# A layer of a hybrid encoder on one core: operand stores issued ahead of the next chunk's loads in mixing, another order of work where the stages of the feed-forward phase change, and POOL making the held operand's sums for the first two blocks of each later stage

## The reference

```python
def mixer(x, mem, w_in, conv_w, conv_b, conv_ln_g, conv_ln_b, pool_w, pool_scale, w_mk, w_mv, w_out):
    h = x @ w_in
    ...
    a = jax.nn.silu(layer_norm(a, conv_ln_g, conv_ln_b))   # GLU, causal depthwise conv of width 31
    p = pool_mixer(p_in, pool_w, pool_scale)
    mo = memory_cross_attention(q, mem, w_mk, w_mv)
    return jnp.concatenate([a, p, mo], axis=-1) @ w_out

def conv_ffn(x, w_up, ffn_conv_w, ffn_conv_b, w_down):
    u = causal_depthwise_conv(x @ w_up, ffn_conv_w, ffn_conv_b)   # width 3
    g = u[..., :D_FF]
    v = u[..., D_FF:]
    return (jax.nn.silu(g) * v) @ w_down                           # D_FF = 2816

x = layer_norm(x, ln0_g, ln0_b)
x = layer_norm(DEEPNORM_ALPHA * x + mixer(x, ...), ln1_g, ln1_b)
x = layer_norm(DEEPNORM_ALPHA * x + conv_ffn(x, ...), ln2_g, ln2_b)
```

## Time and profile before

| | us |
|---|---|
| median of three runs | 2126.25 |
| lowest and highest | 2125.7, 2127.76 |
| the profiled execution | 2126.83 |
| its span, first to last instruction | 2125.1 |
| PE busy in it | 1924.2 (91%) |
| DVE busy | 1627.2 (77%) |
| ACT busy | 984.3 (46%) |
| POOL busy | 220.7 (10%) |

### The profile page before, as it was taken

One profiled execution on the slowest core, in us unless ns is written; L12 is line 12 of the kernel. 1 busy time (PEld: TensorE's weight loads), 2 busy tenths in 40 slices (PEclk: granted clock), 3 DMA queues, 4 the chain that ended last, 5 costly groups with the idle time before them and its releaser, 6 DMA issues.

```text
span 2125.1 us, 26517 instructions
## 1 busy us (share of the span) xinstructions
PE 1924.2 (91%) x8584; PEld 1585.8 (75%) x8584; DVE 1627.2 (77%) x2241; ACT 984.3 (46%) x1681; POOL 220.7 (10%) x263
## 2 busy tenths in 40 slices
PE   4999999679788919999999989999999798998997
PEld 3887877558677717888888768888888586887885
DVE  7979868567677637888888888877778767657897
ACT  4255252554554325555555655555555434324321
POOL 1010100001131210222221002000000000000111
PEclk9999999889899959999999999999999899999998
DMA  6130210523224253333434433322214467557542
GB/s 251 57 119 20 79 40 21 195 75 132 106 104 148 101 217 124 139 135 131 148 138 138 167 131 129 109 89 79 84 74 137 167 216 267 172 175 259 188 165 102
DMA packets 135378, 282.96 MB, mean 133 GB/s; under 512 B 10384, under 2 KB 66832, under 8 KB 135312
## 3 DMA queue, kind: packets, MB, share of 16 engines
q1 hardware_dynamic: 135312, 282.13, 37.4%
HBM read 182.48 MB, written 99.61 MB: 133 GB/s over the span
## 4 chain that ended last, share of the span: by engine, by line
PE 54%; DMA 4%; DVE 3%; ACT 1%; issue 1%; SPq 0%; POOL 0%; DVEq 0%; ACTq 0%; POOLq 0%
PE prod_ps L1662 54%; DVE mov_lo L1837 1%; DMA y_scratch<-up_and_out 1%; ACT mov_hi L1709 1%; DMA mov_raw<-wdown_sums_scratch 1%; DMA mov_raw<-in_w_down 1%; DMA mov_raw<-x_operands 1%; DVE up_and_out L1871 0%; DMA ffn_conv_b<-in_ffn_conv_b 0%; DVE up_and_out L1868 0%; DMA up_and_out<-x_scratch 0%; DVE sta_lo L1833 0%; ACT sta_hi L1702 0%; SPq L1489 0%; DVE sta_raw L1849 0%
## 5 line engine op out<-in xcount | busy, mean ns | idle before, releaser
L1662 PE MATMUL prod_ps<-mov_hi,sta_hi 128*128 128x512 f32 x1848 | 727.8, 394 | 46.1 <-ACT half_sums L1722 22.3
L1662 PE MATMUL prod_ps<-mov_lo,sta_hi 128*128 128x512 f32 x1848 | 725.2, 392 | 0.0
L1662 PE MATMUL prod_ps<-mov_hi,sta_lo 128*128 128x512 f32 x1848 | 724.5, 392 | 0.0
L1662 PEld LDWEIGHTS prod_ps<-mov_hi,sta_hi 128*128 128x128 f32 x1848 | 350.7, 190 | 126.9 <-ACT half_sums L1722 24.7
L1662 PEld LDWEIGHTS prod_ps<-mov_hi,sta_lo 128*128 128x128 f32 x1848 | 350.6, 190 | 73.7
L1662 PEld LDWEIGHTS prod_ps<-mov_lo,sta_hi 128*128 128x128 f32 x1848 | 351.0, 190 | 72.5
L1702 ACT ACTIVATE sta_hi<-sta_raw 128x512 fp32r<-128x512 f32 (+1 forms) x340 | 197.2, 612 | 180.9 <-PE prod_ps L1662 126.5
L1833 DVE TENSOR_TENSOR sta_lo<-sta_raw,sta_hi 128x512 fp32r<-128x512 f32 (+1 forms) x340 | 222.0, 669 | 56.0 <-ACT sta_hi L1702 54.1
L473 DVE SCALAR_TENSOR_TENSOR conv_pool<-glu,conv_w,conv_pool 128x512 f32<-128x512 f32 x240 | 160.1, 749 | 0.0
L294 PE MATMUL wb<-x0t_hi,win_hi 128*128 128x512 f32 x352 | 138.0, 392 | 4.8 <-DVE win_lo L528 4.8
L294 PE MATMUL wb<-x0t_lo,win_hi 128*128 128x512 f32 x352 | 137.9, 392 | 0.0
(11 more groups left out here) (241 smaller groups left out, 2811.3 us busy)
## 6 DMA issues: line engine op xcount, KB each, us to landing
sta_raw<-in_w_up SPq DMA_DIRECT2D x88, 512.0 KB, 4.2
hidden_scratch<-up_and_out SPq DMA_DIRECT2D x44, 512.0 KB, 2.6
y_scratch<-up_and_out SPq DMA_DIRECT2D x16, 1024.0 KB, 7.3
sta_raw<-hidden_scratch SPq DMA_DIRECT2D x32, 512.0 KB, 4.5
up_and_out<-y_scratch SPq DMA_DIRECT2D x16, 1024.0 KB, 4.9
x_operands<-x_operands_out SPq DMA_DIRECT2D x56, 256.0 KB, 4.6
mov_raw<-x_operands SPq DMA_DIRECT2D x14, 1024.0 KB, 6.9
mov_raw<-in_w_down SPq DMA_DIRECT2D x44, 256.0 KB, 4.5
```

Of the source, the lines that this page charges most:

```text
L1662: last = pe.matmul(psum, w, x, start=(start and k == 0 and i == 0), stop=(stop and k == m - 1 and i == 2), skip_group_check=True)
```

## The change

1. Mixing, SP: the operands of chunk c-2 are stored directly behind the load of the residual's first input, ahead of `store_x1` and of the next input load.
2. Mixing, POOL: the operand sums of the chunk before stand ahead of the first rstd, no longer between the two.
3. Feed-forward phase, start: ACT waits for the constants of the convolution before the first tap, no longer before its first copy.
4. Changes of stage, SP: operand 3 is loaded at the head of the last block, ahead of the store of results, and the load of the first residual of stage 2 waits for the taps of the convolution and goes ahead of the last hidden store.
5. Changes of stage, ACT and DVE: operands 1 to 4 are split in the last block, and DVE takes operand 3 first and 4 behind the next block's part 0; ACT keeps `half_sums` between the splits; DVE takes the value tap and `c22` ahead of the gate tap.
6. POOL makes `held_sums` for blocks 0 and 1 of stages 1 to 4. The next held load also waits for the sums.
7. Down stages: `down_c12` stands ahead of `down_c21`. In the last stage, statistics and the scaling by gain are made for each half of a block as it is complete, and each half is stored with a DMA of its own.

```diff
                     if not (isinstance(c, int) and c == 1):
                         store_x1(sp, c - 2, 1)
                     load_x0(sp, c, 0)
+                    if not (isinstance(c, int) and c == 1):
+                        store_operands(sp, c - 2)
                     store_x1(sp, c - 1, 0)
...
                     sp.wait_ge(p_l, c + 1)
                     load_chunk(sp, c + 2, s)
-                if not first and not (isinstance(c, int) and c == 1):
-                    store_operands(sp, c - 2)
                 if not first:
                     load_x0(sp, c, 1)
...
+                if before is not None:
+                    operand_sums(before)
                 pool.wait_ge(ln_var, c * TT + 1)
                 rstd_on_pool(pool, st[:, 0, :], half, step).then_inc(ln_stats, 1)
-                if before is not None:
-                    operand_sums(before)
...
+        def held_sums(eng, b):
+
+            n = num(b) * 4
+            a11, a12, a21, a22 = quadrant(b, 0, 0), quadrant(b, 0, 1), quadrant(b, 1, 0), quadrant(b, 1, 1)
+            eng.wait_ge(raw_in[b.r], (num(b) - b.r) * 16 + 32)
+            if past(b, 1):
+                eng.wait_ge(sta_lo[4], num(b))
+                eng.wait_ge(sta_lo[5], num(b))
+                eng.wait_ge(s_sum, n)
+            eng.tensor_tensor(sums(b, 0), a21, a22, ALU.add).then_inc(s_sum, 1)
+            eng.wait_ge(s_sum, n + 1)
+            eng.tensor_tensor(a21, a11, a21, ALU.subtract).then_inc(s_sum, 1)
+            eng.wait_ge(s_sum, n + 2)
+            eng.wait_ge(sta_lo[0], num(b) + 1)
+            eng.tensor_tensor(a11, sums(b, 0), a11, ALU.subtract).then_inc(s_sum, 1)
+            eng.wait_ge(s_sum, n + 3)
+            eng.tensor_tensor(sums(b, 1), a12, a11, ALU.subtract).then_inc(s_sum, 1)
...
+            return isinstance(b.i, int) and b.st > 0 and b.i < 2
...
+                    sp.wait_ge(s_sum, 4 * num(b) - 4)
...
+                    for e in range(2):
+                        sp.wait_ge(y_tile, (num(b) - BASE[LAST]) * 2 + e + 1)
+                        sp.dma_start(out[bass.ds(b.i * 256 + e * P, P), :], yt[:, b.r, e, :]).then_inc(y_out, 16)
...
+                sp.dma_start(part_d[bass.ds(b.i * 256, 256), :].rearrange("(e p) d -> p e d", p=P), yt[:, b.r, :, :]).then_inc(y_out, 16)
...
+                if ends(b):
+                    load_moving(b.st + 1, 3)
                 if wdown is not None:
                     load_wdown(wdown, b.r)
+                if at(b, BASE[UP_STAGES]):
+                    for w in (GATE, VALUE):
+                        sp.wait_ge(conv_done[w], 2 * FFB)
+                    load_y(b)
                 if before is not None and before.st < UP_STAGES:
...
                     if at(b, BASE[UP_STAGES]):
                         sp.wait_ge(h_stored, 16 * 2 * FFB)
-                        load_y(b)
...
+                        sp.wait_ge(y_out, y_stores(before))
...
                 if ends(b):
-                    for j in (3, 4):
-                        load_moving(b.st + 1, j)
+                    load_moving(b.st + 1, 4)
...
+            with pool.Fori(0, 9) as q:
+                wdown_sums(q)
+            held_sums(pool, Blk(1, 0, 0))
+            held_sums(pool, Blk(1, 1, 1))
+            with pool.Fori(9, FFB // 2) as q:
+                wdown_sums(q)
+            for st in range(UP_STAGES, LAST + 1):
+                held_sums(pool, Blk(st, 0, 0))
+                held_sums(pool, Blk(st, 1, 1))
...
                     if past(b, 1):
                         act.wait_ge(h_stored, num(b) * 16)
+                    else:
+                        act.wait_ge(consts, 32)
...
-                    moving_hi(b.st, 3)
-                    moving_hi(b.st, 4)
-                    if after is not None:
-                        hi(after, 0)
-                    hi(b, 5)
-                    moving_hi(b.st, 5)
-                    hi(b, 6)
-                    moving_hi(b.st, 6)
-                elif at(b, 0):
+                if at(b, 0):
                     hi(b, 5)
                     moving_hi(0, 5)
                     hi(b, 6)
                     moving_hi(0, 6)
-                    hi(after, 0)
                 else:
                     hi(b, 6)
                     hi(b, 5)
-                    if after is not None:
-                        hi(after, 0)
                 if ends(b):
                     moving_hi(b.st + 1, 0)
...
+                    hi(after, 0)
+                if opens(b):
+                    moving_hi(b.st, 5)
+                    keep_u2(b)
...
                     first_tap(before, VALUE)
-                keep_u2(b)
+                if opens(b):
+                    moving_hi(b.st, 6)
+                    keep_u4(b)
+                else:
+                    keep_u2(b)
+                if ends(b):
+                    moving_hi(b.st + 1, 1)
                 if was_up:
...
-                if after is not None:
+                if not opens(b):
+                    keep_u4(b)
+                if ends(b):
+                    hi(after, 1)
+                    moving_hi(b.st + 1, 2)
+                    hi(after, 2)
+                    moving_hi(b.st + 1, 3)
+                    hi(after, 3)
+                    hi(after, 4)
+                    moving_hi(b.st + 1, 4)
+                elif after is not None:
                     for j in (1, 2, 3, 4):
                         hi(after, j)
-                if ends(b):
-                    moving_hi(b.st + 1, 1)
-                    moving_hi(b.st + 1, 2)
...
             act.wait_ge(zeroed, 1)
-            act.wait_ge(consts, 32)
...
+                if past(b, 1):
+                    dve.wait_ge(conv_done[VALUE], num(b))
                 dve.tensor_tensor(tokens(b, VALUE, 1), bank(4 + b.r), u[:, 1, :].rearrange("p (q t) -> p q t", t=P), ALU.add).then_inc(c22, 1)
...
+            def centred(b, e):
+
+                n = (num(b) - BASE[LAST]) * 2 + e
+                if e == 0:
+                    dve.wait_ge(c11, num(b) + 1)
+                    dve.wait_ge(c12, num(b) + 1)
+                else:
+                    dve.wait_ge(c21, num(b) + 1)
+                    dve.wait_ge(u4_added, num(b) - BASE[UP_STAGES] + 1)
+                dve.bn_stats(lst[:, e, 0:6], yt[:, b.r, e, 0:512])
+                dve.bn_stats(lst[:, e, 6:12], yt[:, b.r, e, 512:1024]).then_inc(ln_part, 1)
+                dve.wait_ge(ln_part, n + 1)
+                dve.bn_aggr(lst[:, e, 12:14], lst[:, e, 0:12]).then_inc(ln_var, 1)
+                dve.wait_ge(ln_var, n + 1)
+                dve.wait_ge(gb_loaded, 32)
+                dve.scalar_tensor_tensor(out=yt[:, b.r, e, :], in0=yt[:, b.r, e, :], scalar=lst[:, e, 12:13], in1=g_b[:, 0, :],
+                                         op0=ALU.subtract, op1=ALU.mult).then_inc(ln_scaled, 1)
...
             def finish(b):
-                down_c21(b)
                 down_c12(b)
                 if b.st == LAST:
-                    statistics(b)
+                    centred(b, 0)
+                down_c21(b)
+                if b.st == LAST:
+                    centred(b, 1)
...
                     moving_lo(b.st, 3)
-                    moving_lo(b.st, 4)
                     if after is not None:
                         lo(after, 0)
+                    moving_lo(b.st, 4)
...
+                    if ends(b):
+                        moving_lo(b.st + 1, 0)
                     if after is not None:
                         lo(after, 0)
-                if ends(b):
-                    moving_lo(b.st + 1, 0)
-                if was_up:
+                if was_up and opens(b):
+                    conv(before, VALUE)
+                    if b.st < UP_STAGES:
+                        up_c22(b)
                     conv(before, GATE)
-                    conv(before, VALUE)
+                    if not at_boundary(after):
+                        held_sums(dve, after)
                     gated(before)
-                if after is not None:
...
+                    if after is not None and not at_boundary(after):
+                        held_sums(dve, after)
...
-                if after is not None:
+                if after is not None and not ends(b):
                     lo(after, 1)
...
-                if b.st < UP_STAGES:
+                if b.st < UP_STAGES and not opens(b):
                     up_c22(b)
-                else:
+                if b.st >= UP_STAGES:
                     down_u4(b)
+                if ends(b):
+                    lo(after, 1)
+                    moving_lo(b.st + 1, 1)
+                    lo(after, 2)
+                    moving_lo(b.st + 1, 2)
                 if after is not None:
...
-                if ends(b):
-                    moving_lo(b.st + 1, 1)
-                    moving_lo(b.st + 1, 2)
...
```

72 lines of the change are left out of this document (21 added, 51 removed).

## The result

The changed kernel takes 2090.86 us (median of four runs, 2088.37 to 2092.15); the kernel before, beside it, 2125.97. The ratio is 0.9833, with a 95% interval of 0.9816 to 0.985. So the change is worth 35.1 us, where 47.6 were forecast, and the time lies 3.9 us above the range that was given. The profiled run took 2091.34 us with a span of 2089.5.

A forecast was written before the change was run, and what follows sets the result against it. TensorE, computing for 91% of the span, was taken as the bound, leaving its idle time and lower clock. 34.0 + 9.1 - 1.9 - 0.4 + 1.1 + 0.8 + 4.9 = 47.6 us; median 2078.6, range 2061 to 2087.

The forecast's parts named there:

- The 34.0 us from four chunks at 32.2: Mixing: with stores ahead of the loads, four stalled chunks totalling 162.8 us fall to 32.2 each, winning 34.0 us.
- I cost the delay at nothing: Mixing: rstd late by nothing to 2.3 us behind POOL's moved sums, costed at nothing; uncovered, at most 9 us in four.
- its result is first needed by the affine pair: Mixing: cover for a late rstd, as DVE's affine pair starts some two us after the activation ends.
- In the other blocks of the last stage DVE has the same work in another order: Last stage: 2.5 us more DVE work ahead of three splits with 3 us to spare, costed at nothing.
- the rival of 2064.5: Changes of stage: POOL does not slow taps and splits, so they win 13.8 us and the time is 2064.5; chance 0.25.
- the reading that DVE works at 0.53 to 0.56 of its speed while POOL runs contended: DVE beside POOL: slowing as a rate; four sums of 512 last 8.6 us and cost DVE 3.8 us.
- the terms at the changes of stage: Four changes between feed-forward stages: 1.9 us and 0.4 lost, then 1.1 and 0.8 won.
- The move does not relieve DVE, it costs 1 us: Held sums moved to POOL: cost DVE 3.8 us by contention, against 2.8 if DVE makes them itself.
- The new wait: Changes of stage: PE's second product needs ACT's preset, now behind all five splits, so PE waits for a DMA.
- the new wait is dearer: Rival: each change of stage loses 3 us more, giving 2090.6 us; chance 0.13.
- The start and the end: Feed-forward start: 9.1 us won without the constants' wait; last block: 4.9 us won by half-wise statistics, scaling and stores.
- Between those places PE has no gap: Whole kernel: PE has no gap between mixing, the feed-forward start and the four changes of stage.

The follow-up runs named there:

- experiment 2: Kernel before, with only SP's operand stores in mixing moved ahead of the store of x1 and the next load: 2091.42 us, ratio 0.9837.
- experiment 6: Changed kernel, with gain and bias of the last LayerNorm loaded early, directly behind moving operand 6 in the last stage's first block: 2084.83 us, ratio 0.9809.
- experiment 3: Changed kernel, with each of POOL's four operand sums in mixing made as two instructions of half the size: 2086.94 us, ratio 0.9815.
- experiments 5 and 4: 5: kernel before, with only POOL making held_sums for blocks 0 and 1 of stages 1 to 4, 2132.44 us, ratio 1.0031; 4: see experiment 4.
- experiment 4: Changed kernel, with the held operand's sums of blocks 0 and 1 back on DVE in every stage: 2082.47 us, ratio 0.9793.
- experiments 8 and 9: Changed kernel, with preset ahead of operand 4's split: 2087.05 us; then also DVE's split of operand 4 ahead of the held operand's part 0: 2083.34 us.
- experiment 7: Kernel before, with only ACT's wait for the convolution's constants moved from its first copy to before the first tap: 2119.52 us, ratio 0.9962.
- experiment 1: Changed kernel, with POOL's operand sums in mixing back between the two rstds, SP's stores staying in their new place: 2080.86 us, ratio 0.9785.

## Why the prediction was wrong, and where it was right

**Mixing: the mechanism right, the term mis-sized.** The 34.0 us from four chunks at 32.2 hold for the stores alone, to the tenth (experiment 2). What failed is the step on POOL's move: "I cost the delay at nothing", and "the affine pair loses its neighbour on POOL and gets shorter, which nobody waits for". I priced what the move does to POOL's own chain and to the operations that it leaves. I never asked which operations it goes to. They are four short ones on the way to the attention: L1176, L1147, L1148 and L1149 take 6.24 us in place of 1.95, so DVE is 4.3 us later.

From there the delay goes two ways. On DVE itself 1.1 us fall into idle time, and 2.4 are given back where POOL's sums no longer run (L1182 and the affine pair), so that 0.8 are left. The statistics, though, come 3.6 us later, and with them the rstd. Here the cover of the prediction failed, "its result is first needed by the affine pair": ACT's activation needs it sooner, and ACT's copies for the attention stand behind that activation. They come 2.9 us later, and PE's attention 1.7 (all compared with the same chunk with the stores alone, experiment 2). The rstd is late because DVE's statistics are, not because POOL is still at its sums, which the prediction had priced. Four of the six chunks are 1.7 us longer than with the stores alone, the fifth 1.3, and the last is 0.3 shorter: 7.6 in all. The prediction had rows that show what POOL does to DVE, the affine pair at 2.30 and at 1.23; it had not looked up the neighbours at 623, which were these four.

**Block 1 of stage 4: a wait that was overlooked.** "In the other blocks of the last stage DVE has the same work in another order", which was costed at nothing, failed. The scaling by gain had stood in `normalise`, a block after the statistics; in `centred` it stands with them, and `gb_loaded` is waited for a block sooner. Nobody had moved the load, which SP issues behind two transfers of y. It costs 5.3 us once, since the two tiles are loaded once (experiment 6).

**The two engines slow each other: right in kind, wrong in form.** Taps take 2.31 and 2.17 us beside POOL, over the 2 us that were to confirm it, so the rival of 2064.5 falls. But the reading that DVE works at 0.53 to 0.56 of its speed while POOL runs contended is false. A split of 2.28 us becomes 3.38, not 4.1; an addition of 0.42 becomes 1.56, not 0.8. The loss is about 1.1 us an operation, at any size from 128x256 to 128x2048, which is what is left of POOL's running instruction, and it shrinks with that instruction (experiment 3). For large operations the two readings come out close, 4.1 us against 3.8 for four, and the terms at the changes of stage held (-0.8, -0.1, 1.4 and 2.7 against -1.9, -0.4, 1.1 and 0.8). For short ones they differ by three times, and those were in mixing.

The Trainium skill has the rule that the prediction should have used. "SBUF — State Buffer", section "SBUF: two separate sides", says that the port pair of DVE and GpSimd is an exclusive lock and not a split of bandwidth: of a GpSimd instruction and a DVE instruction in a two-port mode or with two SBUF inputs (these only against a GpSimd instruction that reads SBUF), the one that starts first holds it whole, and the other is blocked. The rows agree: DVE's L1176 ends 0.28 us behind POOL's L804, and L1147 0.54 behind L805.

**"The move does not relieve DVE, it costs 1 us": right in sign.** In the whole kernel it costs 6.0 us in the kernel before and 8.4 in the changed one (experiments 5 and 4). On DVE's own operations it is 1.3 us for the four sums of experiment 4 (4.1 lost against 2.8 saved).

**The new wait: right.** PE waits for `preset` at the second product of all four stages, 4.67, 1.58, 10.21 and 4.18 us. Taking it out is worth 3.8 us with ACT's order alone, 7.5 with DVE's (experiments 8 and 9). The rival "the new wait is dearer" named 2090.6, almost the time measured, but not its cause: it had every change of stage lose 3 us more, and they lost less than forecast.

**The start and the end: right.** 8.9 against 9.1 and 4.9 against 4.9 in the profile of the whole change. The start was also run by itself (experiment 7); the end was not.

**A reading that was wrong, without weight for the sum.** "Between those places PE has no gap" isn't so: in the kernel before PE also waits in the input phase and at the start of mixing, 12.0 and, in eight waits, 15.8 us at L266 and 17.6 at L918, as it does in the changed kernel.

**The range.** It took in the unknown costs of places that had been looked at, and its upper end lay 8.4 us above the forecast. The two terms that failed make 12.9 us and had no width of their own, since each had been costed at nothing with a cover named on one side alone.

## What to carry to other kernels

When work moves to another place on one engine, price three things: the place that it leaves, its own chain, and the operations of the other engines that now run beside it. Between POOL and DVE count instructions, not microseconds: in this kernel each DVE operation with two inputs in SBUF that meets one of POOL's sums waits for its end, so that short DVE operations suffer most, and POOL work is best put where DVE reads PSUM or has one long instruction. A cover is good only if everything that stands behind the late result on its engine is looked at too, not only the first user. When an operation is moved ahead, follow each operand that it waits for back to its load, and ahead of any split that waits for a DMA put what doesn't need it.

## What the runs showed of the hardware

The additions and taps of DVE and POOL's additions exclude each other for a whole instruction: 0.42 us becomes 1.56 and 2.28 becomes 3.38 beside POOL instructions of 1.26 us, and 0.42 becomes 0.84 to 1.01 beside such of 0.74. POOL loses in the same way: its 512-element sum of the held operand lasts 3.12 us (at 1199.23 in the changed kernel) where it meets a split of 2.28 that began at 1198.92. DVE's scaling of `probs`, which has one input tensor, is held up as well (four take 2.91 us beside halves, 1.14 without). Not held up are the reciprocal, L1180 of the changed kernel (1.75 us beside two of POOL's sums in experiment 1, 1.74 without), and additions that read one of their two inputs from PSUM. In the changed kernel L1916 shows both kinds of addition, beside POOL's sums at the start of stage 4: 0.67 us where it reads `prod_ps` in PSUM (at 1936.62) and 1.19 where it reads `half_sums` in SBUF (at 1937.21).
